# Keys left unscaled, decay rows spread per head, TensorE's heads written out, fills redistributed

## What is computed

```
q = l2norm(q) * 128 ** -0.5;  k = l2norm(k)          # x * rsqrt(sum(x*x) + EPS)
g = cumsum(log decay)                                  # per head, direction and token
decay[c, s] = exp(g[c] - g[s])                         # for s up to c
lmat = strict(beta * (k @ k.T) * decay);  a = lmat + 1
u, w = solve(a, v * beta), solve(a, k * beta * exp(g))
attn = (q @ k.T) * decay
# per chunk: v_new = u - w @ S;  o = (q * exp(g)) @ S + attn @ v_new
#            S = S * exp(g_last) + (k * exp(g_last - g)).T @ v_new
o = o_f + flip(o_b);  o = o * rsqrt(mean(o*o) + EPS) * onorm_g * silu(gate)
```

## Time and profile before

| | |
|---|---|
| median of 3 runs | 2528.78 us (2526.75 to 2529.24) |
| the profiled execution | 2532.0 us, its span 2530.2 us |
| granted TensorE clock over the span | 0.971 |
| TensorE matmul busy | 2384.1 us (94%) |
| VectorE busy | 1001.6 us (40%) |
| ScalarE busy | 934.5 us (37%) |
| GpSimd busy | 289.0 us (11%) |

### The profile page before, as it was taken

The page is one execution under the profiler, slowest core; times in us unless marked ns, Lnnn a source line. Parts: engine busy times, 40 slices in busy tenths (PEclk is TensorE's granted clock), DMA queues, the critical chain, the costliest instruction groups (busy, mean ns, idle before and its releaser), DMA issues.

```text
span 2530.2 us, 39569 instructions
## 1 busy us (share of the span) xinstructions
PE 2384.1 (94%) x14398; PEld 1738.1 (69%) x14398; DVE 1001.6 (40%) x2052; ACT 934.5 (37%) x2443; POOL 289.0 (11%) x196
## 2 busy tenths in 40 slices
PE   6989999999999999999999999839999999999994
PEld 3455656566666656565655554329999999999993
DVE  2547574746556575744424523750001000100012
ACT  3154555546364645544421113312232232223212
POOL 0012221202111221201100000000100110101000
PEclk7989999999999999999999999959999999999997
DMA  9511212120201212021333312267887888688864
GB/s 330 212 52 37 67 26 77 26 77 1 74 29 36 67 36 67 1 76 36 136 150 108 114 69 100 83 218 246 292 297 244 278 288 301 232 282 296 280 227 159
DMA packets 196567, 362.53 MB, mean 143 GB/s; under 512 B 8922, under 2 KB 70311, under 8 KB 193355
## 3 DMA queue, kind: packets, MB, share of 16 engines
q1 hardware_dynamic: 190027, 341.77, 38.6%
q0 software_dynamic: 6400, 18.88, 3.0%
HBM read 319.97 MB, written 40.65 MB: 143 GB/s over the span
## 4 chain that ended last, share of the span: by engine, by line
PE 91%; DVE 3%; DMA 2%; ACT 1%; issue 1%; SPq 0%; POOL 0%; DVEq 0%; ACTq 0%; POOLq 0%
PE bank L610 32%; PE bank L2058 20%; PE bank L2072 10%; PE bank L1493 5%; PE bank L1738 5%; PE bank L796 3%; PE bank L1511 2%; PE bank L788 2%; PE bank L865 1%; PE bank L854 1%; PE bank L781 1%; PE bank L870 1%; DMA arena<-in_ada_w 1%; PE bank L845 1%; PE bank L869 1%
## 5 line engine op out<-in xcount | busy, mean ns | idle before, releaser
L610 PE MATMUL bank<-arena 128*128 128x512 f32 (+1 forms) x2496 | 929.9, 498 | 14.8 <-DMA arena<-in_w_in 12.8
L2058 PE MATMUL bank<-arena 128*128 128x144 f32 x4096 | 512.7, 286 | 5.1 <-ACT arena L2091 5.1
L2058 PEld LDWEIGHTS bank<-arena 128*128 128x128 f32 x4096 | 509.4, 190 | 5.3 <-ACT arena L2091 5.3
L610 PEld LDWEIGHTS bank<-arena 128*128 128x128 f32 x2496 | 375.8, 192 | 170.6 <-issue 167.1
L2140 DVE TENSOR_TENSOR arena<-arena,bank 128x144 f32<-128x144 f32 x128 | 38.9, 304 | 706.5 <-ACT arena L2099 706.5
L2072 PE MATMUL bank<-arena 128*128 128x144 f32 x2048 | 257.2, 286 | 0.7 <-DVE arena L2140 0.7
L2072 PEld LDWEIGHTS bank<-arena 128*128 128x128 f32 x2048 | 253.8, 189 | 1.9 <-DVE arena L2140 0.9
L796 PEld LDWEIGHTS bank<-arena 128*128 128x128 f16 x1296 | 98.5, 98 | 170.0 <-issue 156.8
L970 ACT ACTIVATE arena<-bank 128x384 f16<-128x384 f16 (+1 forms) x360 | 160.2, 496 | 141.2 <-PE bank L796 102.8
L2099 ACT ACTIVATE arena<-bank 128x144 f32<-128x144 f32 x128 | 37.3, 291 | 464.1 <-PE bank L2058 464.1
L641 ACT ACTIVATE arena<-bank 128x512 f32<-128x512 f32 (+1 forms) x156 | 76.6, 492 | 252.3 <-PE bank L610 251.9
(11 more groups left out here) (274 smaller groups left out, 2671.8 us busy)
## 6 DMA issues: line engine op xcount, KB each, us to landing
arena<-in_exp_w_gate SPq DMA_DIRECT2D x32, 2048.0 KB, 10.0
arena<-in_exp_w_up SPq DMA_DIRECT2D x32, 2048.0 KB, 15.5
arena<-in_exp_w_down SPq DMA_DIRECT2D x32, 2048.0 KB, 10.6
arena<-in_w_in SPq DMA_DIRECT2D x52, 512.0 KB, 5.0
arena<-in_ada_w SPq DMA_DIRECT2D x24, 1024.0 KB, 7.7
side_dram<-arena SPq DMA_DIRECT2D x20, 576.0 KB, 3.3
arena<-side_dram SPq DMA_DIRECT2D x20, 576.0 KB, 3.9
arena<-g_dram SPq DMA_DIRECT2D x16, 576.0 KB, 4.7
```

Of the source, the lines that this page charges most:

```text
L610: ins = nc.tensor.matmul(unit_bank(order, name)[:, 0:n], w[:, k, :], hT3[:, k, at:at + n], start=(k == 0), stop=(k == KD - 1))
L2058: last = nc.tensor.matmul(banks[3 + f % 2][:, m * CAP:(m + 1) * CAP], w_unit[2 * half + m][:, k, col:col + P], xsT[:, k, :], start=(k == 0 ...
```

## The change

- **k stays unscaled.** The three column-sum matmuls, ScalarE's squares of the whole k, the logarithm and exponential over [128 x 1152] and VectorE's two products are gone. k is transposed first (place "kT"); ScalarE squares it with a sum per token, as q, and copies the transposed k (`squares`); the lengths are columns (`k_log`, `k_rec`). They enter the decay's rows (`g_cols` = g - 0.5 log), the subtracted column (`gcb_k`), the scan's columns (`ndec_k`, `kd_k`) and q's scale (`q_arg`). The bound of the decay's argument is 16 instead of 0.
- **Decay rows per head.** The prologue's decay rows are gone. In each head TensorE transposes three groups of six columns, VectorE copies the rows out, SyncE stores them in `g_dram`, waits for the store, and then spreads them (`load_decays`).
- **q's transposes wait for k's banks**: `USES[0]` begins with k, then q; `USES[1]` with the new rows, then v.
- **The output's sum and square** move from GpSimd to VectorE (sum, ahead of the last convolution tap) and ScalarE (nine squares with sums); ScalarE's copy of the last unit now comes behind the scale and ahead of the gate's SiLU.
- **Fills**: 69 instead of 61 matmuls up to the third "Y2" place, and the last 8 at "end2" are gone. The unit q2 moves ahead of A0 and B0.
- **TensorE's loop** over heads 0 to 6 is written out.

The diff's parts stand in this order: tables, SyncE, TensorE (`body_pe`), ScalarE (`body_act`), VectorE (`body_dve`).

```diff
-        FILLS = {"start": 6, "nk": 5, "qT": 16, "kk": 16, "Y20": 8, "Y21": 8, "Y22": 2, "X0": 1, "X1": 1, "X2": 1, "res": 2, "fix": 4, "end1": 6}
+        FILLS = {"start": 6, "kT": 5, "qT": 29, "kk": 13, "Y20": 6, "Y21": 8, "Y22": 2, "X0": 1, "X1": 1, "X2": 1, "res": 2, "fix": 4, "end1": 6}
-        ORDER = ("q1", "q0", "v0", "k0", "g0", "A0", "B0", "q2", "v1", "v2", "k1", "k2", "g1", "g2", "A1", "A2", "B1", "B2")
+        ORDER = ("q1", "q0", "v0", "k0", "g0", "q2", "A0", "B0", "v1", "v2", "k1", "k2", "g1", "g2", "A1", "A2", "B1", "B2")
-        USES = {0: ["qT", "kT", "kk"], 1: ["nk", "vT", "kq"]}
+        USES = {0: ["kT", "qT", "kk"], 1: ["gT", "vT", "kq"]}
...
+        def load_decays(sp, h):
+            all_drained(sp, h, 1, "gT")
+            sp.dma_start(g_dram[bass.ds(h, 1), :].rearrange("o (g r c) -> (o r) g c", g=3, r=6), g_rows[0:6, :].rearrange("p (g c) -> p g c", g=3)).then_inc(sem("g_saved"), 16)
+            sp.wait_ge(sem("g_saved"), 16 * h + 16)
+            for d in range(2):
+                sp.dma_start(grow[d], g_dram[bass.ds(h, 1), d * T:(d + 1) * T].to_broadcast([P, T])).then_inc(sem(f"head_in{d}"), 16)
...
+            def turn_tokens(d, name, src):
+                for g in range(3):
+                    if name != "kT":
+                        drained(pe, h, d, name, g)
+                    for i in range(3):
+                        last = nc.tensor.transpose(TRI[d][g][:, i * P:(i + 1) * P], src[:, tcol(3 * g + i):tcol(3 * g + i) + P], ident)
+                    last.then_inc(sem(f"filled{d}"), 1)
             fill("start")
             pe.wait_ge(sem("scan_done"), h + 1)
-            pe.wait_ge(sem("sq_ready"), h + 1)
-            for b, (at, n) in enumerate(SPAN):
-                nc.tensor.matmul(TRI[1][b][:, 0:n], ones, k_square[:, at:at + n], start=True, stop=True).then_inc(sem("filled1"), 1)
-            fill("nk")
+            pe.wait_ge(sem("qk_silu"), 2 * h + 1)
+            turn_tokens(0, "kT", kT)
+            fill("kT")
             pe.wait_ge(sem("qk_silu"), 2 * h + 2)
+            turn_tokens(0, "qT", qT)
+            pe.wait_ge(sem("columns"), 5 * h + 2)
             for g in range(3):
+                nc.tensor.transpose(TRI[1][g][0:6, 0:P], g_cols[:, 6 * g:6 * g + 6], ident).then_inc(sem("filled1"), 1)
             fill("qT")
+            pe.wait_ge(sem("v_ready"), h + 1)
+            turn_tokens(1, "vT", vT)
...
+            def squares(name, junk, sums, kept=None):
+                for g in range(3):
+                    filled(act, h, 0, name, g)
+                    for i in range(3):
+                        t = 3 * g + i
+                        last = nc.scalar.activation(junk[:, t * P:(t + 1) * P], TRI[0][g][:, i * P:(i + 1) * P], ACT.Square, accum_out=sums[:, t:t + 1])
+                    if kept is not None:
+                        last = nc.scalar.activation(flat(kept, g), TRI[0][g][:, 0:384], ACT.Copy)
+                    last.then_inc(sem("drained0_act"), 1)
+                all_drained(act, h, 0, name)
+            squares("kT", dm_flat[1], k_rec, ktok)
+            nc.scalar.activation(k_log, k_rec, ACT.Ln, bias=eps_c).then_inc(sem("lengths"), 1)
+            act.wait_ge(sem("lengths"), 3 * h + 1)
+            nc.scalar.activation(k_rec, k_log, ACT.Exp, scale=-0.5).then_inc(sem("lengths"), 1)
+            evac("kT")
+            squares("qT", kq_flat[0], q_norm)
+            nc.scalar.activation(q_norm, q_norm, ACT.Ln, bias=eps_c).then_inc(sem("lengths"), 1)
             evac("qT")
...
-            evac("end1")
+            act.wait_ge(sem("o_added"), h + 1)
+            for t in range(NT):
+                last = nc.scalar.activation(kq[1][:, t, :], kq[0][:, t, :], ACT.Square, accum_out=orow[:, t:t + 1])
+            last.then_inc(sem("o_sumsq"), 1)
             act.wait_ge(sem("o_sumsq"), h + 1)
             nc.scalar.activation(orow, orow, ACT.Ln, scale=1.0 / P, bias=eps_c).then_inc(sem("o_ln"), 1)
             act.wait_ge(sem("o_ln"), h + 1)
             nc.scalar.activation(orow, orow, ACT.Exp, scale=-0.5).then_inc(sem("o_rstd"), 1)
+            evac("end1")
...
-            decay_arguments(0)
-            dve.wait_ge(sem("rnorm"), h + 1)
-            nc.vector.tensor_tensor(kT[:, 0:CTX], kT[:, 0:CTX], k_square[:, 0:CTX], ALU.mult)
-            nc.vector.tensor_tensor(kT[:, LAT0:LAT0 + LAT], kT[:, LAT0:LAT0 + LAT], k_square[:, CTX:T], ALU.mult).then_inc(sem("k_normed"), 1)
-            decay_arguments(1)
+            dve.wait_ge(sem("lengths"), 3 * h + 1)
+            for d in range(2):
+                nc.vector.scalar_tensor_tensor(g_cols[:, d * NT:(d + 1) * NT], k_log, -0.5, of_head("gc", d), ALU.mult, ALU.add).then_inc(sem("columns"), 1)
+            for d in range(2):
+                nc.vector.scalar_tensor_tensor(gcb_k[d], k_log, 0.5, of_head("gcb", d), ALU.mult, ALU.add).then_inc(sem("columns"), 1)
+            dve.wait_ge(sem("lengths"), 3 * h + 2)
+            for d in range(2):
+                nc.vector.tensor_tensor(ndec_k[d], k_rec, of_head("ndec", d), ALU.mult)
+                nc.vector.tensor_tensor(kd_k[d], k_rec, of_head("kd", d), ALU.mult)
+            for g in range(3):
+                filled(dve, h, 1, "gT", g)
+                nc.vector.tensor_copy(g_rows[0:6, g * P:(g + 1) * P], TRI[1][g][0:6, 0:P]).then_inc(sem("drained1_dve"), 1)
+            dve.wait_ge(sem("lengths"), 3 * h + 3)
+            nc.vector.tensor_tensor(q_arg, q_norm, k_log, ALU.subtract).then_inc(sem("columns"), 1)
...
+            dve.wait_ge(sem("columns"), 5 * h + 4)
+            for d in range(2):
+                decay_arguments(d)
```

More of the change, by code:

```diff
@@ L176, in build @@
         q_norm = take(NT)
+        k_log, k_rec, q_arg = take(NT), take(NT), take(NT)
+        g_cols = take(2 * NT)
+        gcb_k, ndec_k, kd_k = [take(NT) for _ in range(2)], [take(NT) for _ in range(2)], [take(NT) for _ in range(2)]
+        g_rows = take(3 * P)
         scan = dm_flat[0][:, 0:6 * P].rearrange("p (s d c) -> p s d c", s=3, d=2)
@@ L355, in pe_decay_sums @@
             nc.tensor.matmul(banks[5][:, 2 * NT * H:4 * NT * H], ones, tab["g"].rearrange("p t d -> p (t d)"), start=True, stop=True).then_inc(*reach("gsum_filled"))
-        def pe_decay_rows(pe):
-            pe.wait_ge(*at_step("gc_ready"))
-            for t in range(NT):
-                last = nc.tensor.transpose(banks[2 + t // 3][0:2 * H, (t % 3) * P:(t % 3 + 1) * P], tab["gc"][:, t, :], ident)
-            last.then_inc(*reach("gT_filled"))
         def pe_shift2(pe):
@@ L482, in dve_decay_rows @@
             nc.vector.tensor_tensor(tab["kd"], tab["kd"], tab["beta"], ALU.mult)
-            dve.wait_ge(*at_step("gT_filled"))
-            for b in range(3):
-                last = nc.vector.tensor_copy(gT_rows[0:2 * H, b * 384:(b + 1) * 384], banks[2 + b][0:2 * H, 0:384])
-            last.then_inc(*reach("gT_ready"))
         def dve_part(dve, g):
@@ L517, in build @@
         USES[0] += ["oT"]
-        BY_DVE = {(d, n) for d in range(2) for n in ["vT", "kk", "res", "oT", "fix"] + [f"P{b}" for b in LEVELS]}
+        BY_DVE = {(d, n) for d in range(2) for n in ["gT", "vT", "kk", "res", "oT", "fix"] + [f"P{b}" for b in LEVELS]}
         def use(d, name):
@@ L952, in body_act @@
                 nc.scalar.activation(dm_flat[d], dm_flat[d], ACT.Exp).then_inc(sem("decay_exp"), 1)
+            act.wait_ge(sem("columns"), 5 * h + 5)
+            nc.scalar.activation(q_norm, q_arg, ACT.Exp, scale=-0.5, bias=qscale_c)
             act.wait_ge(sem("b_out"), 16 * h + 16)
@@ L1356, in _ @@
             if stop >= 4:
-                with pe.Fori(0, H - 1) as h:
+                for h in range(H - 1):
                     body_pe(pe, h)
```

86 lines of the change are left out of this document (20 added, 66 removed).

## The result

| | before | changed |
|---|---|---|
| median | 2528.99 us (4 runs, 2526.75 to 2529.24) | 2551.57 us (4 runs, 2548.37 to 2552.65) |
| ratio with its 95% interval | | 1.0083 (1.0071 to 1.0095) |
| the profiled execution, its span | 2532.0, 2530.2 us | 2552.65, 2550.9 us |
| from one head's output transposes to the next's, inner heads | 140.5 us | 143.1 us, 144.5 in two of six |

What follows compares the result with a forecast made beforehand. TensorE's own work was taken to bound each head; less work (-1.6 us) against new waits (4.25) replacing old ones (0.9) gave +1.8 per inner head. Six inner heads +11, first -0.8, last +1.6: +12, so 2541 us, range 2523 to 2563.

Steps and rivals of the forecast that it cites:

- last head: Period of the last head: 1.6 us longer.
- Column sums out, transposes in (-1.6): TensorE's work per head: column sums of 1.94 us go, three transposes of 0.33 come, net -1.6 us.
- Output norm, 0.6: At the output norm only 7 matmuls, not 15, cover the chain, so TensorE waits 0.6 us.
- q's transposes behind k's squares, 2.4: q's transposes wait for ScalarE to square and copy k out of shared banks: 2.4 us, the largest term.
- The third fill unit at q, 0.55: Among the fills at q, k's unit waits 0.55 us for a bank whose copy stands behind q's squares.
- The first triangle, 0.5: At the end of the decay chain TensorE waits 0.5 us for the first triangle.
- Waits of before that these replace, about 0.9: Old waits at the head boundary that the new ones replace: 46.5 us less 45.6 of work.
- First head, -0.8: First head 0.8 us shorter: the 2.4 at q shrinks to 0.3 and no output norm precedes.
- The store's round trip: Decay rows: 3.2 us store, covered by 0.7; rival at 8.6 gives 2579, chance 0.09 together with several larger waits.
- The clock rival: Clock falls near q's transposes: +2.2 us more in up to seven heads, up to 2556; chance 0.13.
- Written-out program, zero: TensorE's loop written out: no gap at the loop's head boundary, so nothing to win; fetch-stall rival chance 0.02.
- The faster rival, "the cover holds": TensorE stays full at q's transposes if ScalarE reaches k's squares 2.5 us sooner: about 2519 us; chance 0.20.

Runs made afterwards that it cites:

- e9: Changed kernel with the output's sum and squares back on GpSimd and the reduction on VectorE: 2572.47 us.
- e7: Changed kernel with ScalarE's squares and copies of k ahead of v's SiLU and the table load: 2569.22 us.
- e6_select: Changed kernel with GpSimd's first select held back until VectorE has made all 18 decay arguments: 2549.53 us.
- e4_tri: Changed kernel with VectorE's two triangle copies put ahead of v's copies: 2542.43 us.
- e8_all: Changed kernel with gate SiLU and triangle copies earlier, select held back, v's SiLU later and one fill moved to the output norm: 2521.87 us.
- e10_fills_back: Changed kernel with the fill numbers and unit sequence of the kernel before: 2581.45 us.
- e3_args: Changed kernel with decay arguments made by the two-input form instead of the one-input form: 2550.28 us.
- e11: Changed kernel with 10 fills instead of 5 between k's and q's transposes and 24 instead of 29 behind them: 2541.45 us.
- e2_gate: Changed kernel with ScalarE's copy of the last unit put back behind the gate's SiLU: 2541.8 us.
- e5: Kernel before with TensorE's loop over heads 0 to 6 written out: 2530.41 us against 2530.93, ratio 0.9997.
- e1: Changed kernel with TensorE's loop over heads 0 to 6 put back: 2558.69 us.

## Why the prediction came out as it did

The account of the span, from the starts of the output transposes (281.89, 426.43, 569.53, 712.65, 855.76, 1000.14, 1143.25, 1307.32 us; before 280.19, 420.67 and so on every 140.5, then 1286.32):

| | forecast | measured |
|---|---|---|
| start of the first head | 0 | +1.0 |
| first head | -0.8 | +0.7 |
| six inner heads | 6 x 1.8 = +11 | 6 x 2.6 = +15.7 |
| clock falls | a rival | 2 x 1.3 = +2.6 |
| last head | +1.6 | +1.0 |
| sum | +12 | +21 |

**Column sums out, transposes in (-1.6): right.** The sums took 1.94 us from start to start (567.45, and the next fill starts at 569.39), the new transposes 0.33 (582.66 to 582.99).

**Output norm, 0.6: right,** 0.66 in the bracket, 0.8 from start to start. That the sum had to go from GpSimd to hold it there is e9's 3.9.

**q's transposes behind k's squares, 2.4: right.** ScalarE's first square was worked out as 15.6 us behind the last scan step (563.9 less 548.29); it came at 15.55. The transposes ended at 582.2, 3.2 us after TensorE was ready at 579.1, and 1.0 of that is work: 2.2. Three waits in the rows sum to 1.55; the rest lies between records. What e7 adds is that the shared banks aren't the cause, only the first place where it shows.

**New columns, 0.2: right in the bracket** (0.24), 0.45 from start to start. **The third fill unit at q, 0.55: wrong,** none: 29 narrow fills took 6.5 us from start to start (582.99 to 589.49), all of it work. The copy that frees its bank (585.44 to 585.7) ended 23.0 us behind the last scan step; it had been worked out at 23.6.

**The first triangle, 0.5: too small, and the largest miss,** 1.23 in the bracket and 1.35 from start to start. The chain was marched right up to its start (VectorE free 30.1 us behind the last scan step; measured 592.74 less 562.70, 30.0) and right behind it, except for one step: "arguments to 580.3 and 582.2", 3.8 us for 18. They took 4.7. Their price came from a row where nothing ran on GpSimd, and the change puts them beside the first select. e6_select shows this cause; e4_tri shows the wait going when 1.4 us are taken from the chain. This price, 3.8 for 4.7, is the step of the working that failed.

**"Waits of before that these replace, about 0.9": 0.6 of it was there.** How much pure work the stretch from the last scan step to the first level product holds can be read from e8_all: there it takes 44.9 us (548.87 to 593.78) and has one gap, 0.6 at the new columns, so 44.3 is work. The changed kernel's 49.1 then hold 4.8 of waits (0.8, 2.2, 0.45, none at the third unit, 1.35), where the forecast had 4.25. The kernel before has 1.6 more work, 45.9 of its 46.5, so 0.6 of waiting in rows that show none. A row of the timeline hides a short wait inside a run of fills; the view of the fill's line, over q's fills (572.7 to 576.7), shows it:

```profile
L610 PE MATMUL bank<-arena x32: 275/275/377, 572.8 to 576.5; 128*128 128x128 f32 x32
...
  ACT arena L641: 0.2, 1
```

TensorE waits 0.2 us there for a unit's copy: these 16 narrow fills take 3.87 us from start to start (3.64 to 3.99 in the eight heads), and 3.60 in e10_fills_back (447.53 to 451.13). So 4.8 less 0.6 less 1.6 is the measured 2.6; the forecast had 4.25 less 0.9 less 1.6. Of the 0.8 between them about 0.5 is new waits that were longer (the triangle by 0.85, the new columns by 0.25, the output norm by 0.2, less 0.2 at q and the 0.55 that never came), and 0.3 is a remainder that was taken for waiting and was small differences of price.

**First head, -0.8: wrong.** Its 2.4 at q did vanish as forecast. But the output norm's 0.6 was taken off for the head ahead of it, while the period ends with its own output transposes and holds 0.66. With 0.8 there, 1.35 at its triangle and 0.6 at its columns, less 1.6 of work and the 0.6 that an inner head before had waited (above), it is about +0.55.

**The store's round trip: hidden, as forecast,** and shorter: 1.4 us, not the 3.2 taken from the output's store. The rival of a long one fell.

**The clock rival: partly true.** It was given 0.13 and "up to seven heads"; two heads had it, at +1.3 each (fills of 6.67 us took 7.87). The Trainium skill (TensorE: Matmul & The Clock Gate, "HAM oscillation") says that a burst followed by a wait loses the clock each time anew. The trace agrees on the fall itself, and e9 shows it in every head behind waits of 3.9 us and e7 in four of six behind 3 us; but with three waits in 3 us it came in two heads of six, in e3_args in one, in e6_select in three, in e4_tri in five, and in e11 (0.61) and e2_gate (0.21 and 0.61) in none. What picks the heads where the waits are the same stays open. It also means that a wait removed elsewhere (e4, e6) can be given back here.

**Written-out program, zero: right for the kernel before (e5), wrong for the changed one (e1),** where it saves about 7 us. As the diff contains it, it entered the forecast with the right value; as a cause it was misjudged.

**The prologue, zero: 1.0 us later.** The first head starts at 138.94 instead of 137.96, with the same wait for the same weights (13.11 for 12.83). In the profiles of the experiments, with the same prologue, the first head began between 136.7 and 139.2, so it can be the spread between executions. It wasn't tested further.

The faster rival, "the cover holds", asked for k's first square before about 561.5 on the old axis; it came at 563.9 as worked out. e8_all is that rival made true by hand, and at 2522 close to its 2519.

## What to carry to other kernels

When an engine is full, the price of a change is the removed work minus the waits that appear where other engines' chains are now too long for the cover: march both chains from a common start, and take every new wait from start to start. A remainder between priced work and elapsed time may be waiting that a merged row hides or only small differences of price (here 0.6 and 0.3 of 0.9): ask for the view of that line before it enters the sum. Each price has to come from a row with the same neighbours: VectorE work that moves beside GpSimd, or a jump that moves behind a wait, has another price. And when waits are shown to move with the order on a side engine, reorder that engine before giving up the change: the same algorithm went from 22.6 us slower to 9 us faster.

## What the runs showed of the hardware

- A 128x128 VectorE subtract-and-minimum of 280 ns took 1299 to 1306 ns, once in each of eight heads, beside GpSimd's 1.26 us select, and at most 293 with the select held back. With a second SBUF input it took 344 to 352 always, and the select took 1.99 us instead of 1.26. The Trainium skill (SBUF — State Buffer, "Who interferes with whom") says that the two engines share a pair of ports, that the first form can hold both for its whole length, the second contends for reading, and whichever comes second is blocked. The traces agree on both, with the loser changing from VectorE to GpSimd.
- TensorE stood still for 4.42 us at one of six jumps back of a loop, with no releaser in the trace and DMA share 0.83, and at none in the kernel before, which has no wait there. Two packets of the instruction queue lie where the stop begins and none behind the other five jumps. That TensorE was waiting for instructions is likely, not shown: the kernel before has such a packet behind its jumps too, without a stop.
- The small store of the decay rows, [6 x 384], 9 KB, released its waiter 1.4 us after the issue; 64 KB of output had taken 3.2.
- The clock's lower level (1.2 GHz) came in one to five of six equal-looking heads, depending on the kernel, with waits of 0.41, 0.54 and 0.60 us (in e4_tri TensorE was busy 1.11 of the 2 us in which it fell); it cost 1.3 us in a stretch of narrow fills.
